# Gate/up stage of a transformer layer: a fourth seven-product pair, and one chunk split by a GpSimd DMA

## The chip, the cores and the metric

One core of a Trainium2 chip runs the whole layer as one program. The metric is the device time of one execution in microseconds. The engines are TensorE (PE; its weight loads are shown as PEld), VectorE (DVE), ScalarE (ACT), GpSimd (POOL) and SyncE (SP, here only the issuer of loads). They run side by side and wait for each other on semaphores.

## What is computed

The reference, cut to the stages that matter here. There are 256 tokens (two blocks of 128), D = 2048 and D_FF = 5632, all in float32.

```python
x = x + y @ w_out                       # out stage, y from the token mixing
h = rms_norm(x, ffn_norm)
x = x + (silu(h @ w_gate) * (h @ w_up)) @ w_down
return rms_norm(x, final_norm)
```

## The kernel before

**Products.** Every float32 operand is split in two: `hi`, its value rounded by a copy into a reduced float32 form, and `lo`, what is left. A product of 128 x 128 by 128 x 512 is three matmuls: hi by hi, hi by lo, lo by hi (`group`, L1571).

**Chunks and blocks.** Weights stream in chunks of 1 MB, `[128, 4, 512]`. The gate/up stage is 11 blocks (`FS`, index i), one for each 512 hidden columns; a block is 8 chunks (`FB`, index p), one for each pair of 128-row tiles of D. A chunk holds two row tiles of the up and of the gate matrix. The down stage has 44 chunks of the same size. Chunks are counted in one numbering, the gate/up stage from `FF0` and the down stage from `DN0`.

**Plain and seven-product chunks.** A plain chunk (`plain_chunk`) is 8 products, 24 matmuls, into the four PSUM banks 0 to 3: bank 2 up + b for token block b and matrix up or gate. A chunk in `SUMS` = 0, 2, 4 (`sums_chunk`) treats its four blocks as a 2 x 2 block product by the seven-product scheme, 21 matmuls. It needs four sums of weight blocks (`t_sum`, three DVE instructions), their hi and lo parts (`t_hi` by ACT, `t_lo` by DVE) beside the chunk's own three blocks, and seven blocks of x and its sums in place of four. Its shared products collect in banks 4 to 7. After the last chunk of `SUMS` these are combined (`mix_sums`) and added into banks 0 and 1, then 2 and 3 (`mix_banks(i, 0, ..)` and `mix_banks(i, 1, ..)`).

**Order in a block.** The matmuls of chunk `SUMS[-1]` signal `mix_done`; the plain chunk after it (5) does banks 0 and 1 first and signals `part_done`, and `mix_banks(i, 0)` waits for that; `mix_banks(i, 1)` waits for that chunk's end. Chunk 6 waits for `mixed` before each half. The last chunk ends the banks one by one (`ffn_done`). ACT turns banks 0 and 1 into `silu` (L811), DVE multiplies with banks 2 and 3 (L1354, the gate products). PE transposes the 128 x 512 results four tiles at a time (`hidden_turn`, L1463): the first group after the next block's chunk 0, the second after a quarter of its chunk 1. ACT copies each group into `hid` (`keep_hidden`, L769); the second group waits for the first copy.

**Preparation.** Each engine works through its list in order. At step p of block i ACT (`prep_hi`) and DVE (`prep_lo`) prepare chunk p + 3 (`AHEAD`): ACT makes `w_hi` from `raw` (and `t_hi` once the sums exist); DVE makes, for a plain chunk, `w_lo` = raw - w_hi (L1159), and for a sums chunk three sums (L1167, L1170, L1172), `w_lo` of three blocks (L1177) and `t_lo` (L1180). On DVE `mix_sums` and `mix_banks(i, 0)` stand at the head of step 4, `mix_banks(i, 1)` at the head of step 5, the gate products at the head of step 7. In the last block, steps 5 to 7 prepare the first chunks of the down stage (`down_lo`, L1296 to L1332). So at the end of a block DVE's list is: first bank mix, chunk 7, second bank mix, next chunk 0, next chunk 1, gate products, next chunk 2.

**Loads.** SP issues one load for a chunk into one of four buffers (`RING`), chunk n into `raw[n % 4]`, once chunk n - 4 is used (`chunk_used`, counted by PE). `w_lo` overwrites `raw`. `lo_ready` tells PE that a chunk is prepared. The residual x lies in `xin` (16 KB of each partition) from the in stage to the end; the out stage adds to it, `residual` reads it late in each half of the down stage. SP, DVE and ACT run the middle blocks in loops (`Fori`), PE too; out and down stage are written out.

## Time and profile before

| | us |
|---|---|
| median of 3 runs (1095.08 to 1096.28) | 1096.15 |
| the profiled execution, its own time | 1096.81 |
| its span, first to last instruction | 1095.1 |
| PE busy | 1084.2 |
| DVE busy | 886.2 |
| ACT busy | 617.8 |
| gate/up stage, by the chain | 387.56 to some 855 |

The span and the profiled execution's own time differ by 1.7 us, which lie around the program. PE's matmuls overlap in the record: each is shown with 0.39 us, but one starts every 0.23 us, so starts are what to read. In a timeline a row is one instruction or several alike; the bracket at its end is the idle time before it, with what ended it. Instructions on one engine can overlap by about 0.1 us, so the cost in a sequence is from one start to the next. In the chain in order of time a piece is a stretch of work on one engine and line.

### The profile page before, as it was taken

What the parts mean: (1) busy time and instruction counts of PE and PEld (TensorE: products, weight loads), DVE (VectorE), ACT (ScalarE), POOL (GpSimd) and SP (SyncE); (2) the same over time, 40 slices, a digit from 0 to 9 for tenths busy, and PEclk for the clock granted to TensorE, in tenths of its full rate; (3) what the DMA queues carried; (4) which work ended last, traced back from release to release, by engine and by line L of the source; (5) the groups of instructions that cost most, each with busy time, mean ns of one, the idle gap of its engine ahead of it and who ended that gap; (6) DMA issues with size and microseconds to landing.
All of it is one profiled execution on the core that took longest, in us unless ns stands there. A gap on an engine that the chain in (4) does not pass through costs nothing.

```text
span 1095.1 us, 13280 instructions
## 1 busy us (share of the span) xinstructions
PE 1084.2 (99%) x5127; PEld 902.5 (82%) x5127; DVE 886.2 (81%) x822; ACT 617.8 (56%) x616; POOL 44.5 (4%) x44
## 2 busy tenths in 40 slices
PE   9999999999999999999999999999999999999997
PEld 6888889987888888888888888888888888878886
DVE  7879666754576789898898898888898898989994
ACT  7666546655755655464554555554554765555553
POOL 0077000000000000000000000000000000000000
PEclk9999999999999999999999999999999999999999
DMA  8765644654355555555555555555555655555552
GB/s 329 282 232 194 199 137 124 202 159 147 118 192 169 178 197 211 200 198 192 192 194 198 208 189 207 192 192 196 198 214 197 230 193 197 202 194 204 202 193 114
DMA packets 48550, 212.57 MB, mean 194 GB/s; under 512 B 4096, under 2 KB 9984, under 8 KB 28544
## 3 DMA queue, kind: packets, MB, share of 16 engines
q1 hardware_dynamic: 47648, 209.65, 54.9%
q10 hardware_dynamic: 864, 2.39, 0.6%
q8 instruction: 27, 0.44, 0.2%
q14 instruction: 11, 0.09, 0.0%
HBM read 209.93 MB, written 2.10 MB: 194 GB/s over the span
## 4 chain that ended last, share of the span: by engine, by line
PE 96%; DVE 1%; DMA 1%; ACT 1%; issue 0%; SPq 0%; DVEq 0%
PE ps L1571 73%; PE ps L1424 6%; PE ps L1426 6%; PE ps L1425 6%; PE ps L1463 2%; DMA raw<-in_w_dn 1%; PE ps L1511 1%; PE ps L1688 1%; PE ps L1689 1%; PE ps L1690 1%; PE ps L1510 0%; DMA raw<-in_w_i 0%; DVE w_lo L1296 0%; ACT t_hi L788 0%; ACT w_hi L781 0%
## 5 line engine op out<-in xcount | busy, mean ns | idle before, releaser
L1571 PE MATMUL ps<-w_hi,xp_hi 128*128 128x512 f32 x539 | 211.7, 393 | 0.0
L1571 PE MATMUL ps<-w_hi,xp_lo 128*128 128x512 f32 x539 | 210.0, 390 | 0.0
L1571 PE MATMUL ps<-w_lo,xp_hi 128*128 128x512 f32 x539 | 209.7, 389 | 0.0
L887 DVE TENSOR_TENSOR w_lo<-raw,w_hi 128x2048 fp32r<-128x2048 f32 (+2 forms) x42 | 87.3, 2078 | 85.5 <-ACT w_hi L444 85.5
L1159 DVE TENSOR_TENSOR w_lo<-raw,w_hi 128x2048 fp32r<-128x2048 f32 x55 | 125.8, 2288 | 34.4 <-ACT w_hi L692 34.4
L692 ACT ACTIVATE w_hi<-raw 128x2048 fp32r<-128x2048 f32 x55 | 105.1, 1910 | 62.1 <-DMA raw<-in_w_gu 62.1
L781 ACT ACTIVATE w_hi<-raw 128x2048 fp32r<-128x2048 f32 (+1 forms) x44 | 79.2, 1800 | 80.0 <-DMA raw<-in_w_dn 79.9
L700 ACT ACTIVATE t_hi<-t_sum 128x2048 fp32r<-128x2048 f32 x33 | 63.4, 1920 | 100.0 <-DVE t_sum L1172 100.0
L1571 PEld LDWEIGHTS ps<-w_hi,xp_lo 128*128 128x128 f32 x539 | 101.1, 188 | 21.5
L1571 PEld LDWEIGHTS ps<-w_lo,xp_hi 128*128 128x128 f32 x539 | 101.3, 188 | 20.4
L1571 PEld LDWEIGHTS ps<-w_hi,xp_hi 128*128 128x128 f32 x539 | 101.2, 188 | 20.1
L1571 PE MATMUL ps<-w_hi,xo_hi 128*128 128x512 f32 x292 | 114.0, 390 | 0.4 <-DVE xin L1385 0.4
L1571 PE MATMUL ps<-w_lo,xo_hi 128*128 128x512 f32 x292 | 113.6, 389 | 0.0
L1571 PE MATMUL ps<-w_hi,xo_lo 128*128 128x512 f32 x292 | 113.6, 389 | 0.0
L444 ACT ACTIVATE w_hi<-raw 128x2048 fp32r<-128x2048 f32 (+2 forms) x42 | 73.0, 1738 | 49.5 <-DMA raw<-in_w_out 25.6
L1296 DVE TENSOR_TENSOR w_lo<-raw,w_hi 128x2048 fp32r<-128x2048 f32 x32 | 73.2, 2288 | 8.7 <-ACT w_hi L781 8.7
L1180 DVE TENSOR_TENSOR t_lo<-t_sum,t_hi 128x2048 fp32r<-128x2048 f32 x33 | 75.7, 2293 | 3.8 <-ACT t_hi L700 1.0
L696 ACT ACTIVATE w_hi<-raw 128x1536 fp32r<-128x1536 f32 x33 | 49.2, 1491 | 37.5 <-DMA raw<-in_w_gu 37.1
L1571 PEld LDWEIGHTS ps<-w_hi,xo_hi 128*128 128x128 f32 x292 | 54.8, 188 | 12.7 <-DVE xin L1385 0.8
L1571 PEld LDWEIGHTS ps<-w_hi,xo_lo 128*128 128x128 f32 x292 | 54.8, 188 | 11.4
L1571 PEld LDWEIGHTS ps<-w_lo,xo_hi 128*128 128x128 f32 x292 | 54.8, 188 | 11.1
L1571 PE MATMUL ps<-w_hi,xT_hi 128*128 128x512 f32 x156 | 60.9, 390 | 1.2 <-DVE w_lo L1017 1.0
(280 smaller groups left out, 2188.1 us busy)
## 6 DMA issues: line engine op xcount, KB each, us to landing
raw<-in_w_gu SPq DMA_DIRECT2D x88, 1024.0 KB, 4.8
raw<-in_w_dn SPq DMA_DIRECT2D x44, 1024.0 KB, 4.8
raw<-in_w_i SPq DMA_DIRECT2D x21, 1024.0 KB, 4.8
raw<-in_w_out SPq DMA_DIRECT2D x16, 1024.0 KB, 5.0
raw<-in_w_in SPq DMA_DIRECT2D x12, 1024.0 KB, 5.0
raw<-in_w_in SPq DMA_DIRECT2D x8, 576.0 KB, 3.8
raw<-in_w_i SPq DMA_DIRECT2D x6, 512.0 KB, 6.8
raw<-in_w_ukv SPq DMA_DIRECT2D x3, 1024.0 KB, 5.1
```

The source lines that it names most:

```text
L444: nc.scalar.activation(w_hi[n % 4][:, 0:k, 0:c], raw[n % 4][:, 0:k, 0:c], ACT.Copy).then_inc(hi_ready, 1)
L692: nc.scalar.activation(w_hi[slot][:], raw[slot][:], ACT.Copy).then_inc(hi_ready, 1)
L700: nc.scalar.activation(t_hi[s % 2][:], t_sum[s % 2][:], ACT.Copy).then_inc(tops_hi, 1)
L781: nc.scalar.activation(w_hi[slot][:, blocks, :], raw[slot][:, blocks, :], ACT.Copy).then_inc(hi_ready, 1)
L887: nc.vector.tensor_tensor(w_lo[n % 4][:, 0:k, 0:c], raw[n % 4][:, 0:k, 0:c], w_hi[n % 4][:, 0:k, 0:c].bitcast(F32), ALU.subtract).then_inc ...
L1159: nc.vector.tensor_tensor(w_lo[slot][:], raw[slot][:], w_hi[slot][:].bitcast(F32), ALU.subtract).then_inc(lo_ready, 1)
L1180: nc.vector.tensor_tensor(t_lo[s][:], t_sum[s][:], t_hi[s][:].bitcast(F32), ALU.subtract).then_inc(lo_ready, 1)
L1296: nc.vector.tensor_tensor(w_lo[slot][:], raw[slot][:], w_hi[slot][:].bitcast(F32), ALU.subtract).then_inc(lo_ready, 1)
L1424: nc.tensor.matmul(out, hi, w_h, start=start, stop=False)
L1425: nc.tensor.matmul(out, hi, w_l, start=False, stop=False)
L1426: return nc.tensor.matmul(out, lo, w_h, start=False, stop=stop)
L1571: mm = nc.tensor.matmul(out, x, wt, start=start and j + m == 0, stop=stop and 3 * j + m == n - 1, skip_group_check=resumed)
```

## The change

- `SUMS` becomes 0, 2, 4, 5. The last sums chunk is 5, chunk 6 is the one with `part_done`, and chunk 7 waits for `mixed` and ends the banks, all four in the order 0, 1, 2, 3. The sums of x for pair 5 are made in the out stage, with a fourth step in `XS_SPLIT`.
- Chunk 7 leaves the ring of four buffers and the lists of `prep_hi` and `prep_lo`. SP loads it into `d_raw` (`load_apart`, behind the load of chunk 3; in block 0 behind that of chunk 5). ACT (`prep_apart`, after step 2; in block 0 after step 3) copies it into `d_hi` and writes the negated `d_hi` over `d_raw`, in two halves, as `d_lo`. GpSimd then adds the same weights from DRAM onto `d_lo` by two accumulating DMAs of 512 KB, and PE waits for both (`lo_added`). Ring positions come from `ring(n)`, and a load waits for the last user of its buffer (`slot_user`).
- `d_lo` and `d_hi` lie on `xin`. SP writes x (2 MB) to `x_keep` in DRAM in block 0, behind the load of chunk 3, and reads it back in the down stage behind the load of its chunk 3; `residual` waits for `x_back`.
- On DVE `mix_sums` and `mix_banks(i, 0)` stand at step 5, then come the sums of the next chunk 0, `mix_banks(i, 1)`, and the low parts of that chunk. In the last block the whole `down_lo(0)` stands between the two. Chunk 5's sums wait for chunk 2's use.
- All loops of the stage are written out. Index arithmetic in `prep_*`, `down_*` and the PE functions follows `ring(n)`; it is left out below, as are the moved addresses of small tiles.

```diff
-SUMS = (0, 2, 4)
+SUMS = (0, 2, 4, 5)
 NS = len(SUMS)
+BY_DMA = 7
...
-for _step, _pairs in ((58, (0, 1)), (59, (2, 3)), (62, (4, 5)), (FF0, (6, 7))):
...
+for _step, _pairs in ((58, (0, 1)), (59, (2, 3)), (62, (4,)), (63, (5,)), (FF0, (6, 7))):
     put(_step, *(("xs2" if _pair in SUMS else "xt2", _pair) for _pair in _pairs))
-XS_SPLIT = {59: 0, 60: 1, 63: 2}
+XS_SPLIT = {59: 0, 60: 1, 63: 2, 64: 3}
...
+def ring(n):
+
+    return n - sum(FF0 + BY_DMA + FB * i < n for i in range(FS))
...
+def slot_user(n):
+
+    r = ring(n) - RING
+    return next(m for m in range(n) if ring(m) == r and not (FF0 <= m < DN0 and (m - FF0) % FB == BY_DMA))
...
+        d_raw = at("d_raw", 96 * K, [KC, COLS])
+        d_lo = at("d_lo", 96 * K, [KC, COLS], F32R)
+        d_hi = at("d_hi", 104 * K, [KC, COLS], F32R)
...
-            with sp.Fori(0, FS) as i:
+            def load_ring(n, src):
+
+                sp.wait_ge(chunk_used, slot_user(n) + 1)
+                sp.dma_start(raw[ring(n) % 4][:].rearrange("p a b -> p (a b)").unsqueeze(1), src).then_inc(raw_in[ring(n) % 4], 16)
...
+            def load_apart(i):
+
+                if i == 0:
+                    sp.wait_ge(x_kept, 16)
+                    sp.wait_ge(unit_filled, len(ORDER))
+                    sp.wait_ge(nx2.squared, 8)
+                else:
+                    sp.wait_ge(chunk_used, FF0 + FB * i)
+                sp.dma_start(d_raw[:].rearrange("p a b -> p (a b)").unsqueeze(1),
+                             w_gu[:, FB * i + BY_DMA:FB * i + BY_DMA + 1, :]).then_inc(d_in, 16)
+
+            for i in range(FS):
                 for p in range(FB):
-                    load_rows(i * FB + (FF0 + p), (FF0 + p) % 4, w_gu[:, bass.ds(i * FB + p, 1), :])
-            with sp.Fori(0, HKT // 4) as i:
-                for p in range(4):
-                    load_rows(i * 4 + (DN0 + p), (DN0 + p) % 4, w_dn[:, bass.ds(i * 4 + p, 1), :])
+                    if p != BY_DMA:
+                        load_ring(FF0 + FB * i + p, w_gu[:, FB * i + p:FB * i + p + 1, :])
+                    if i == 0 and p == 3:
+                        sp.wait_ge(acc_free, ACC_O + 8)
+                        sp.dma_start(t["x_keep"], xin[:].rearrange("p a b -> p (a b)")).then_inc(x_kept, 16)
+                    if p == (5 if i == 0 else 3):
+                        load_apart(i)
+            for m in range(HKT):
+                load_ring(DN0 + m, w_dn[:, m:m + 1, :])
+                if m == 3:
+                    sp.wait_ge(chunk_used, DN0)
+                    sp.dma_start(xin[:].rearrange("p a b -> p (a b)"), t["x_keep"]).then_inc(x_back, 16)
...
+            for i in range(FS):
+                for half in range(2):
+                    pool.wait_ge(negated, 2 * i + half + 1)
+                    pool.dma_start(d_lo[:, 2 * half:2 * half + 2, :].rearrange("p a b -> p (a b)"),
+                                   w_gu[:, FB * i + BY_DMA, 2 * COLS * half:2 * COLS * (half + 1)],
+                                   accum_op=ALU.add).then_inc(lo_added, 16)
...
+            def prep_apart(i):
+
+                act.wait_ge(d_in, 16 * (i + 1))
+                nc.scalar.activation(d_hi[:], d_raw[:], ACT.Copy).then_inc(d_hi_made, 1)
+                act.wait_ge(d_hi_made, i + 1)
+                for half in (slice(0, 2), slice(2, 4)):
+                    nc.scalar.activation(d_lo[:, half, :], d_hi[:, half, :].bitcast(F32), ACT.Copy,
+                                         scale=-1.0).then_inc(negated, 1)
...
-                    if p == 4:
+                    if p == SUMS[-1]:
...
-                            act.wait_ge(ffn_done, i * 3 + (2 * b + 1))
+                            act.wait_ge(ffn_done, i * 3 + (b + 1))
...
-                    else:
+                    elif p + AHEAD != BY_DMA:
                         prep_hi(i, p + AHEAD)
+                    if p == (3 if first else 2):
+                        prep_apart(i)
...
-            with act.Fori(1, FS - 1) as i:
+            for i in range(1, FS - 1):
...
                 if "s" in parts:
-                    dve.wait_ge(raw_in[slot], i * (4 * FB) + 16 * (n // 4 + 1))
+                    dve.wait_ge(raw_in[slot], 16 * (r // 4 + 1))
+                    if p == SUMS[-1]:
+                        dve.wait_ge(chunk_used, i * FB + (FF0 + SUMS[1] + 1))
...
-                    if p == 4:
+                    if p == SUMS[-1]:
                         mix_sums(i)
                         mix_banks(i, 0, None)
-                    if p == 5:
-                        mix_banks(i, 1, i * FB + (FF0 + 6))
                     if p == FB - 1:
                         for b in range(TOK):
                             dve.wait_ge(gate_set, i * 2 + (b + 1))
                             if b == 0:
-                                dve.wait_ge(ffn_done, i * 3 + 2)
+                                dve.wait_ge(ffn_done, i * 3 + 3)
                             else:
                                 dve.wait_ge(chunk_used, i * FB + (FF0 + FB))
                             nc.vector.scalar_tensor_tensor(out=gate[:, b, :], in0=bank[2 + b],
@@ -1356,7 +1419,13 @@
                                                            op0=ALU.mult, op1=ALU.mult).then_inc(hid_made, 1)
                     if last and p + AHEAD >= FB:
                         down_lo(p + AHEAD - FB)
-                    else:
+                        if p == SUMS[-1]:
+                            mix_banks(i, 1, i * FB + (FF0 + 7))
+                    elif p == SUMS[-1]:
+                        prep_lo(i, p + AHEAD, "s")
+                        mix_banks(i, 1, i * FB + (FF0 + 7))
+                        prep_lo(i, p + AHEAD, "l")
+                    elif p + AHEAD != BY_DMA:
...
                 if half == 0:
                     dve.wait_ge(mix_step, 3 * i + 3)
+                    dve.wait_ge(x_back, 16)
...
-                slot = (FF0 + p) % 4
+                w_h, w_l = (d_hi, d_lo) if p == BY_DMA else (m[ring(FF0 + FB * i + p) % 4] for m in (w_hi, w_lo))
...
-                sides = ((0, 0), (1, 0), (0, 1), (1, 1)) if p in (5, 6) else ((0, 0), (0, 1), (1, 0), (1, 1))
+                sides = ((0, 0), (1, 0), (0, 1), (1, 1)) if p > SUMS[-1] else ((0, 0), (0, 1), (1, 0), (1, 1))
                 for g, (b, up) in enumerate(sides):
                     if p == 1 and g == 1:
                         sums_chunk(i, 0, True, late=True) if first else hidden_turn(i, 1)
                     if p == 1 and g == 3:
                         if not first:
                             pe_.wait_ge(hid_kept, i * 2)
-                    if p == 6 and g % 2 == 0:
+                    if p == SUMS[-1] + 2 and g % 2 == 0:
                         pe_.wait_ge(mixed, i * 2 + (g // 2 + 1))
                     toks = slice(b * P, (b + 1) * P)
                     cols = (1, 3) if not up else (0, 2)
                     mm = group(bank[2 * up + b], [xp_hi[p][:, j, toks] for j in range(2)],
-                               [xp_lo[p][:, j, toks] for j in range(2)], [w_hi[slot][:, j, :] for j in cols],
-                               [w_lo[slot][:, j, :] for j in cols], p == 1 and g == 3, p in (5, FB - 1), resumed=p > 5)
-                    if p == 5 and g == 1:
+                               [xp_lo[p][:, j, toks] for j in range(2)], [w_h[:, j, :] for j in cols],
+                               [w_l[:, j, :] for j in cols], p == 1 and g == 3, p > SUMS[-1], resumed=p == SUMS[-1] + 2)
+                    if p == SUMS[-1] + 1 and g == 1:
                         mm.then_inc(part_done, 1)
...
-                    pe_.wait_ge(lo_ready, i * FB + (FF0 + p + 1))
+                    if p == BY_DMA:
+                        pe_.wait_ge(lo_added, 32 * (i + 1))
+                    else:
+                        pe_.wait_ge(lo_ready, ring(FF0 + FB * i + p) + 1)
```

## Rows read from the trace of the kernel before

**Rows 1.** The page, the chain that ended last, by engine.

```profile
PE 96%; DVE 1%; DMA 1%; ACT 1%; issue 0%; SPq 0%; DVEq 0%
```

**Rows 2.** The chain in order of time: start us, us, what.

```profile
519.77 0.44 PE ps L1463 x4
...
522.11 40.15 PE ps L1571 x177
...
562.26 0.44 PE ps L1463 x4
...
862.17 93.20 PE ps L1571 x411
```

**Rows 3.** Timeline of PE: start us, us, engine, line, operation, count.

```profile
1.25 4.90 PE L1561 MATMUL ps<-warm 128*128 128x512 bf16 x14 [1.25 <-DVE warm L922]
...
541.02 0.39 PE L1571 MATMUL ps<-w_hi,xp_hi 128*128 128x512 f32 x1
...
557.34 0.39 PE L1571 MATMUL ps<-w_hi,xp_hi 128*128 128x512 f32 x1
```

**Rows 4.** Windows: us, busy time of each engine, granted clock, DMA share, GB/s.

```profile
10.00:20.00 10.00, 10.00 (x46) 8.29 (x45) 7.39 (x9) 7.61 (x11) 0.00 (x0) 1.00 1.04 409
510.00:550.00 40.00, 40.00 (x182) 32.98 (x181) 34.76 (x26) 20.92 (x16) 0.00 (x0) 1.00 0.56 200
1088.00:1089.00 1.00, 0.17 (x1) 0.00 (x0) 0.07 (x1) 0.69 (x2) 0.00 (x0) 1.00 0.72 279
1090.00:1091.00 1.00, 0.00 (x0) 0.00 (x0) 0.68 (x1) 0.72 (x1) 0.00 (x0) 0.59 0.00 0
```

**Rows 5.** Waits, 429 to 856 us: who waited for whom, us, times, longest.

```profile
PEld ps L1463 <- ACT hid L769: 2.9, 10, 0.3
```

**Rows 6.** Timeline of DVE, out stage and gate/up stage.

```profile
371.96 2.29 DVE L887 TENSOR_TENSOR w_lo<-raw,w_hi 128x2048 fp32r<-128x2048 f32 x1 [3.14 <-ACT w_hi L444]
...
406.94 2.29 DVE L1159 TENSOR_TENSOR w_lo<-raw,w_hi 128x2048 fp32r<-128x2048 f32 x1
...
543.94 1.23 DVE L1283 TENSOR_TENSOR ps<-ps,mix 128x1024 f32<-128x1024 f32 x1 [1.14 <-PE ps L1571]
...
547.28 1.23 DVE L1283 TENSOR_TENSOR ps<-ps,mix 128x1024 f32<-128x1024 f32 x1
548.41 1.22 DVE L1167 TENSOR_TENSOR t_sum<-raw 128x1024 f32<-128x1024 f32 x1
...
550.39 0.69 DVE L1172 TENSOR_TENSOR t_sum<-t_sum,raw 128x512 f32<-128x512 f32 x1
...
555.28 2.29 DVE L1159 TENSOR_TENSOR w_lo<-raw,w_hi 128x2048 fp32r<-128x2048 f32 x1
557.48 1.40 DVE L1354 SCALAR_TENSOR_TENSOR gate<-ps,stats,gate 128x512 f32<-128x512 f32 x2
```

**Rows 7.** Timeline of DVE, last gate/up block, where it prepares the down stage.

```profile
846.00 1.22 DVE L1307 TENSOR_TENSOR t_sum<-raw 128x1024 f32<-128x1024 f32 x1
...
849.57 1.75 DVE L1325 TENSOR_TENSOR w_lo<-raw,w_hi 128x1536 fp32r<-128x1536 f32 x1
851.24 0.68 DVE L1327 TENSOR_TENSOR xo_lo<-hid,xo_hi 128x512 fp32r<-128x512 f32 x1
...
854.65 2.28 DVE L1296 TENSOR_TENSOR w_lo<-raw,w_hi 128x2048 fp32r<-128x2048 f32 x1
```

**Rows 8.** Timeline of ACT at the same block boundary as rows 6.

```profile
561.50 1.92 ACT L700 ACTIVATE t_hi<-t_sum 128x2048 fp32r<-128x2048 f32 x1 [2.92 <-DVE t_sum L1172]
563.32 0.58 ACT L769 ACTIVATE hid<-ps 128x512 f32 x1
```

**Rows 9.** The page, DMA issues: count, KB each, median us to landing.

```profile
raw<-in_w_gu SPq DMA_DIRECT2D x88, 1024.0 KB, 4.8
...
raw<-in_w_i SPq DMA_DIRECT2D x6, 512.0 KB, 6.8
...
xin<-in_x SPq DMA_DIRECT2D x2, 1024.0 KB, 7.0
```

More of the change, by code:

```diff
@@ L141, in build @@
             offset += 2 * size
-        H0 = 153 * K
+        H0 = 156 * K
         assert offset <= H0
@@ L686, in prep_hi @@
             def prep_hi(i, q, parts="bt"):
-                slot, p = (FF0 + q) % 4, q % FB
+                r, p = ring(FF0 + FB * i + q), q % FB
+                slot = r % 4
                 if "b" in parts:
-                    act.wait_ge(raw_in[slot], i * (4 * FB) + 16 * ((FF0 + q) // 4 + 1))
+                    act.wait_ge(raw_in[slot], 16 * (r // 4 + 1))
                 if p not in SUMS:
@@ L776, in down_hi @@
             def down_hi(m):
-                n, q, slot = DN0 + m, m % DQ, (DN0 + m) % 4
-                act.wait_ge(raw_in[slot], 16 * (n // 4 + 1))
+                r, q = ring(DN0 + m), m % DQ
+                slot = r % 4
+                act.wait_ge(raw_in[slot], 16 * (r // 4 + 1))
                 blocks = slice(1, 4) if q in DSUMS else slice(0, 4)
@@ L1367, in _ @@
             ffn(0, first=True)
-            with dve.Fori(1, FS - 1) as i:
+            for i in range(1, FS - 1):
                 ffn(i)
@@ L1742, in sums_chunk @@
                     if first and not late:
-                        after(unit_act, "a", ("xt2", 5))
-                        after(unit_dve, "v", ("xt2", 5))
+                        after(unit_act, "a", ("xs2", 5))
+                        after(unit_dve, "v", ("xt2", 3))
                     elif not first:
@@ L1807, in _ @@
             ffn(0, first=True)
-            with pe_.Fori(1, FS) as i:
+            for i in range(1, FS):
                 ffn(i)
@@ L1965 @@
         t[name] = nc.dram_tensor(f"in_{name}", a.shape, mybir.dt.from_np(a.dtype), kind="ExternalInput").ap()
+    t["x_keep"] = nc.dram_tensor("x_keep", (P, TOK * D), F32, kind="Internal").ap()
     t["out"] = nc.dram_tensor("out_0", (1, TOK * P, D), F32, kind="ExternalOutput").ap()
```

30 lines of the change are left out of this document (17 added, 13 removed).

## The prediction

> **What bounds the kernel now.** I read the page first, then the chain in order of time, the windows, the waits of the gate/up stage, and the timelines of TensorE (PE), VectorE (DVE) and ScalarE (ACT) over one block. By the chain that ended last PE is the bound, with 96% of it [rows 1]. In order of time, one gate/up block is four pieces, two of them transposes, the largest 177 matmuls in 40.15 us, and the next block begins 42.49 us after it [rows 2]. One matmul thus takes 40.15/177 = 0.2268 us. Chunk 5 starts at 541.02 and the next block's chunk 0 at 557.34 [rows 3]: three plain chunks in 16.32 us, 5.44 each; a seven-product chunk of 21 matmuls takes 4.76.
>
> How much room do the others have? In a stretch of 40 us DVE is busy 34.76 and ACT 20.92 [rows 4]. An average hides the order, so I look at the waits: ten times, at every block boundary, the second group of hidden-layer transposes (L1463) waits up to 0.3 us for ACT's copy `hid` (L769) [rows 5]. That is the one chain of this stage with no room at all: DVE's gate product, DVE's three sums for chunk 2, ACT's `t_hi`, ACT's `hid` copy, PE's second turn. It sits where the change puts DVE's work later.
>
> **The matmuls removed.** Chunk 5 of 11 blocks goes from 24 matmuls to 21: 33 x 0.2268 = 7.5 us off the path.
>
> **DVE's total.** Start to start, a sums chunk costs DVE 6.87 us (548.41 to 555.28), a plain one 2.20 (555.28 to 557.48) [rows 6]. The change adds the sums chunk 5 and takes away the plain chunks 5 and 7: 6.87 - 4.40 = 2.5 us more. Before, a block needs 3 x 6.87 + 5 x 2.20 + some 5 for the mixes + 1.3 for the gates = 37.9; after, 40.4 of 41.8 us. As a total that fits. The order decides.
>
> **The order, before.** DVE's first bank mix starts at 543.94, 2.92 us into chunk 5, released by the end of that chunk's first half [rows 3, 6]. I call this the event. From there DVE has no gap: bank mix 1.13, chunk 7's split 2.20, bank mix 1.13, sums chunk 0 6.87, plain chunk 1 2.20; the two gate products start at 557.48 [rows 6], 13.54 us after the event. The event lies 16.32 - 2.92 = 13.40 us before the next chunk 0, so the gates start 0.14 us after it.
>
> **The order, after.** The last sums chunk is now 5 and the event lies in chunk 6, 10.88 - 2.92 = 7.96 us before the next chunk 0. DVE then has: bank mix 1.13; the next chunk 0's sums, 1.98 for the first two (548.41 to 550.39) and 0.60 for the third (0.69 less the 0.09 by which followers overlap), 2.58; bank mix 1.13; chunk 0's low parts, 1.67 (849.57 to 851.24, the same form without a wait) + 2.20 = 3.87; plain chunk 1 2.20 [rows 6, 7]. Sum 10.91: the gates start 2.95 us after the next block's nominal start, **2.8 us later** than before. The work in the chain fell by 2.6 us, its start moved by a whole chunk of 5.44.
>
> **What the 2.8 us meets.** Chunk 0's low parts end 8.8 us after the event, where PE wanted them at 7.96: it waits 0.9 us there. Then the tight chain: from the gates' start to the `hid` copy it is 5.84 us (557.48 to 563.32) [rows 6, 8], with no room [rows 5]. So the whole 2.8 us lands in front of PE's second turn, the 0.9 being part of it and some 2 us a second gap. Does DVE catch up before the next event? From the gates it needs 1.3 + 6.87 + 2.20 + 6.87 + 6.87 + 2.20 = 26.3 us and ends 29.3 us after the nominal start of chunk 0; chunk 6 starts at 2.8 + 41.8 - 10.9 = 33.7. Yes, so the delay doesn't grow. What is late next, behind the turn, is nothing. Ten boundaries: **10 x 2.81 = +28.1 us**.
>
> **The last block.** Here the code doesn't part the sums from the low parts: `down_lo(0)` runs whole between the two bank mixes. It took from 846.00 to 854.65, 8.65 us [rows 7], but behind both mixes. Now the second mix ends 1.13 + 8.65 + 1.23 = 11.0 us after the event, and PE needs it for the second half of chunk 7, at 2.52 + 2.72 = 5.24. PE stands still for **5.8 us**, once. The down stage can't give it back: its first chunks had no PE wait before.
>
> **The clock.** At the tail PE's last matmul ends at 1088.17 (0.17 us busy in that window); between 1090 and 1091 the granted clock is 0.59, on its way from 2.4 to 1.2 GHz [rows 4]. A gap of 5.8 us should lose the clock too. To get it back I take the start: 14 matmuls of 512 columns took 4.90 us [rows 3] against 14 x 0.2268 = 3.18: **+1.7 us**. For the boundary gaps I take none; that is rival (a).
>
> **The first block.** Chunk 5's sums follow chunk 4's on DVE, at 406.94 [rows 6]; with 6.87 and the overlap they end at 413.9, where chunk 5 would start at 557.34 - 3 x 42.49 - 16.32 = 413.5: **+0.4**. In the SP queue 2 MB of x go to DRAM ahead of the loads of chunks 4 to 6, from about 388 on. At 409 GB/s, the most in a window [rows 4], that is 5 us and hidden; at twice the 7.0 us of 1 MB of x [rows 9] it is 14 us, chunk 4's load lands near 405 and it costs up to 5. I take the first: one transfer with long rows, like the weight loads, which land in 4.8 us.
>
> **Costed at nothing.** GpSimd's accumulating DMA: no row shows one. ACT's work for it stands behind chunk 5's `t_hi`. Counted from chunk 6's start, DVE begins chunk 5's sums at 13.8 + 1.3 + 6.87 + 2.20 + 6.87 = 31.1; `t_hi` ends at 31.1 + 2.7 + 1.9 = 35.7 [rows 8], `d_hi` at 37.6, the first negation near 38.7; PE wants the next chunk 7 at 44.6 + 5.4 = 50.1, 11.4 us later. From below, 1 MB lands in 4.8 us; from above, two transfers of 512 KB in series take 2 x 6.8 = 13.6 [rows 9]. Even that is 2.2 us late, and up to 2.8 us at chunk 7 only shorten the gap behind it. So 0, and free up to 14 us. Nothing is queued behind GpSimd's waits. ACT's added work, about 1.9 for `d_hi`, 2.2 for two negations and 1.9 for another `t_hi`, lies beside its idle half; its nearest cover is chunk 6's split behind it, with 0.6 us left. The written-out loops: 177 matmuls took 40.15 in a loop, 411 took 93.20 in the straight down stage [rows 2], both 0.2268: 0. Pair 5's sums of x give DVE and ACT 1 to 2 us more in the out stage, where DVE waited 3.14 us at one step [rows 6]: 0. Reading x back: 0, at most 4 if it takes 14 us and holds up a load of the down stage. DVE's new wait for chunk 2 ends over 1 us before DVE gets there.
>
> The Trainium skill, "DMA: Bandwidth & Descriptors", "Anatomy of one DMA", gives a GpSimd DMA some 2 us plus its bytes over 436 GB/s. That makes an estimated 3.2 us for a half, and the sum stays as it is; no run here shows one yet.
>
> **The sum.** -7.5 + 28.1 + 5.8 + 1.7 + 0.4 = +28.5. On the profiled execution's 1096.8 that is 1125.3; the median of the runs lies 0.66 lower: **1125**.
>
> **Rivals.** (a) The clock falls at every boundary gap as well. For: it was going some 2 us into the tail. Against: matmuls part the 0.9 from the 2. Price 10 x 1.7 = 17: **1142**. (b) The accumulating DMA is slow. Its halves have 14 us; each microsecond beyond costs 11 in all, so at 18 us **1169**. Against: the DMA engines are used 0.56 in this stage [rows 4]. (c) The other side, faster: DVE reaches the gates in time. It decides at 8.1 us from the event to the gates in place of 10.9; then only the matmuls count, 1096.2 - 7.5 = **1089**. For: DVE's total fits. Against: DVE would have to be a quarter quicker than its rows. (d) Turn and copy have slack I don't see and hide half: -7.5 + 14 + 7.5 + 0.4, **1111**.
>
> The Trainium skill, "SBUF — State Buffer", section "SBUF: two separate sides", says that GpSimd can't write descriptors while DVE runs in a two-port mode, which would be a road to (b). The same page says that two-input subtractions have no such mode, and DVE's rows here are of that kind, so (b) stays small.
>
> **Chances.** Forecast 0.68, (a) 0.13, (b) 0.07, (c) 0.07, (d) 0.05. The forecast's own range is 1120 to 1135: below, no clock loss and 0.3 us less at each boundary; above, +5 and +4 for the two transfers of x. To hold 8 in 10 it must reach to (a): 1116 to 1142. A measurement of this kernel tells about 0.2% from no change. Faster 0.07, same 0.01, slower 0.92.
>
> **What would show it.** Right: about 2 us of PE idle before the second turn, ended by ACT `hid`, and 0.9 before chunk 0, ended by DVE `t_lo`; one gap near 5.8 us in the last block, ended by DVE's bank mix; blocks of 44.6 us against 42.49; and only there a lower granted clock. Wrong: blocks of 41.8 us, or PE waiting at chunk 7 for GpSimd's DMA. The prediction falls if the gates start within 0.3 us of the next chunk 0.

## The result and the profile after

The changed kernel takes 1152.7 us in the median of 4 runs (1150.75 to 1156.22), beside 1095.88 for the kernel before on the same chip: a ratio of 1.0522, 95% interval [1.0500, 1.0545], some 57 us slower. (A ratio here is always the kernel's time over that of the kernel before, and the brackets behind it are its 95% interval.) The forecast was 1125, with 1116 to 1142 as the range. The direction was right, but half the size was missing: the time is some 11 us above the range. The profiled execution of the changed kernel has a span of 1150.7 us.

From the page of the changed kernel: busy time by engine, the chain that ended last, and of the DMA part the two queues (packets, MB, share of 16 engines) and one issue (count, KB each, median us to landing).

```profile
PE 1098.2 (95%) x5094; PEld 906.2 (79%) x5094; DVE 911.0 (79%) x858; ACT 653.4 (57%) x650; POOL 69.8 (6%) x66
...
PE 64%; DVE 10%; ACT 10%; DMA 9%; issue 6%; POOL 1%; SPq 0%; DVEq 0%; ACTq 0%
...
q1 hardware_dynamic: 47936, 213.84, 54.6%
q0 software_dynamic: 3168, 11.54, 5.6%
...
d_lo<-in_w_gu POOLq DMA_DIRECT2D x22, 512.0 KB, 8.2
```

PE had 96% of the chain before [rows 1]; now it has 64, and all the others stand in it. No total but PE's is near full, and PE's 95% overstates it, since its matmuls overlap in the record and some ran at the lower clock (below). A chain that runs through every engine while none of the others is full suggests a loop: each waits for the one before it. The waits of the gate/up stage, 429 to 932 us, say who (us in total, times, longest; a selection, not in the order of the view):

```profile
PE ps L1641 <- DMA d_lo<-in_w_gu: 37.6, 11, 5.6
PEld ps L1641 <- DVE w_lo L1221: 7.9, 10, 0.8
PE ps L1641 <- DVE w_lo L1221: 3.6, 10, 0.4
POOL d_lo L480 <- issue: 38.6, 5, 7.9
PE ps L1641 <- DVE ps L1347: 0.3, 1, 0.3
PEld ps L1533 <- ACT hid L818: 0.2, 1, 0.2
```

The wait on which most of my sum stood, PE's second turn for ACT's `hid` (L1533, the line of [rows 5] in the old numbering), is there once, with 0.2 us. In its place PE waits for the accumulating DMA in each of the 11 blocks. Blocks, from chunk 7 to chunk 7, are some 47 us in the second half of the stage (716.59 to 763.49 is one) and 46.8 to 49.9 in the first; all ten take 475.3 us (428.54 to 903.81). I had 44.6 for one; before they were 42.49 [rows 2].

The chain in order of time over one block (start us, us, what; pieces of `issue` of 0.02 us are left out without a mark), with the DMA and chunk 7 of the block behind it:

```profile
683.55 0.45 PE ps L1533 x4
684.03 0.60 ACT hid L818
684.63 1.81 ACT w_hi L741
...
686.46 2.29 DVE w_lo L1221
688.75 1.15 DVE t_sum L1231
...
695.53 1.23 DVE t_sum L1231
...
698.24 1.92 ACT t_hi L749
700.16 1.81 ACT d_hi L845
701.99 1.07 ACT d_lo L848
703.06 0.38 issue
703.44 0.85 POOL d_lo L480
704.29 12.25 DMA d_lo<-in_w_gu
716.54 0.04 issue
716.59 10.52 PE ps L1641 x45
...
728.94 0.45 PE ps L1533 x4
...
749.75 7.86 issue
757.61 5.84 DMA d_lo<-in_w_gu
...
763.49 12.00 PE ps L1641 x45
```

Read it as a circle: PE's second turn, ACT's second `hid` copy, ACT's `w_hi` of chunk 3 queued behind it, DVE's split of chunk 3, the sums of chunks 4 and 5, `t_hi`, `d_hi`, the first negation, GpSimd's issue, 12.25 us of DMA, chunk 7, and PE's second turn again. From turn to chunk 7 it takes 716.59 - 683.39 = 33.2 us (the turn's start in PE's timeline), from there to the next turn 12.2. Together that is 45.4 us, the period of this block: a lateness on the circle comes round to the engine that was late, so nothing absorbs it.

The block behind it shows two things that make the circle longer. GpSimd's second half is issued only after 7.86 us of `issue`, that is, of waiting for nothing that the profile shows. And the 45 matmuls from chunk 7 on take 12.00 us in place of 10.52, because the first of them run at a lower clock.

### The profile page after: what moved, and what is told of

The parts are those of the page before. It is cut to its first block, busy times and chain, and to the rows that moved or that the text cites. A ratio compares the mean times of both kernels' runs of the same rounds, so it can differ in the third digit from the quotient of the medians.

```text
span 1150.7 us, 12406 instructions
## 1 busy us (share of the span) xinstructions
PE 1098.2 (95%) x5094; PEld 906.2 (79%) x5094; DVE 911.0 (79%) x858; ACT 653.4 (57%) x650; POOL 69.8 (6%) x66
## 3 DMA queue, kind: packets, MB, share of 16 engines
q0 software_dynamic: 3168, 11.54, 5.6%
## 4 chain that ended last, share of the span: by engine, by line
PE 64%; DVE 10%; ACT 10%; DMA 9%; issue 6%; POOL 1%; SPq 0%; DVEq 0%; ACTq 0%
PE ps L1641 43%; DMA d_lo<-in_w_gu 8%; PE ps L1494 5%; PE ps L1496 5%; PE ps L1495 5%; ACT t_hi L749 4%; DVE w_lo L1221 3%; DVE t_sum L1231 2%; ACT w_hi L741 2%; PE ps L1533 2%; ACT d_hi L845 2%; DVE t_sum L1236 1%; DVE t_sum L1234 1%; ACT d_lo L848 1%; POOL d_lo L480 1%
## 5 line engine op out<-in xcount | busy, mean ns | idle before, releaser
L1641 PE MATMUL ps<-w_hi,xp_hi 128*128 128x512 f32 x396 | 157.4, 397 | 4.2 <-DVE w_lo L1221 3.6
L1641 PE MATMUL ps<-w_lo,xp_hi 128*128 128x512 f32 x396 | 154.5, 390 | 0.0
L1641 PE MATMUL ps<-w_hi,xp_lo 128*128 128x512 f32 x396 | 154.4, 390 | 0.0
L1221 DVE TENSOR_TENSOR w_lo<-raw,w_hi 128x2048 fp32r<-128x2048 f32 x33 | 75.5, 2289 | 51.4 <-ACT w_hi L741 51.4
L1641 PEld LDWEIGHTS ps<-w_hi,xp_hi 128*128 128x128 f32 x396 | 74.3, 188 | 23.5 <-DVE w_lo L1221 7.9
L1361 DVE TENSOR_TENSOR w_lo<-raw,w_hi 128x2048 fp32r<-128x2048 f32 x32 | 73.2, 2286 | 12.3 <-ACT w_hi L831 12.3
L1641 PE MATMUL ps<-d_hi,xp_hi 128*128 128x512 f32 x88 | 42.2, 480 | 37.9 <-DMA d_lo<-in_w_gu 37.6
L1241 DVE TENSOR_TENSOR w_lo<-raw,w_hi 128x1536 fp32r<-128x1536 f32 x44 | 77.3, 1756 | 1.1
L1641 PE MATMUL ps<-t_hi,xp_hi 128*128 128x512 f32 x176 | 68.5, 389 | 0.4 <-DVE xp_lo L1190 0.4
L1641 PE MATMUL ps<-t_hi,xp_lo 128*128 128x512 f32 x176 | 68.5, 389 | 0.0
L1641 PE MATMUL ps<-t_lo,xp_hi 128*128 128x512 f32 x176 | 68.5, 389 | 0.0
```

Of the source, the lines that this page charges most:

```text
L1221: nc.vector.tensor_tensor(w_lo[slot][:], raw[slot][:], w_hi[slot][:].bitcast(F32), ALU.subtract).then_inc(lo_ready, 1)
L1241: nc.vector.tensor_tensor(w_lo[slot][:, 1:4, :], raw[slot][:, 1:4, :], w_hi[slot][:, 1:4, :].bitcast(F32), ALU.subtract)
L1361: nc.vector.tensor_tensor(w_lo[slot][:], raw[slot][:], w_hi[slot][:].bitcast(F32), ALU.subtract).then_inc(lo_ready, 1)
L1641: mm = nc.tensor.matmul(out, x, wt, start=start and j + m == 0, stop=stop and 3 * j + m == n - 1, skip_group_check=resumed)
```

## The experiments

The kernel before, measured again beside each run, took 1095.5 to 1096.5 us. In the code, `...` marks what is left out.

### Without the accumulating DMA

```diff
-                for half in range(2):
-                    pool.wait_ge(negated, 2 * i + half + 1)
-                    pool.dma_start(d_lo..., w_gu..., accum_op=ALU.add)
...
-                        pe_.wait_ge(lo_added, 32 * (i + 1))
+                        pe_.wait_ge(negated, 2 * (i + 1))
```

> The changed kernel without GpSimd's two accumulating DMAs; PE waits for the negation instead. Left out: chunk 7's low part is only -hi, so that chunk's product is wrong. Theory A (the DMA, 13.5 us from the first negation to the data, lies in a closed loop turn 2, hid copy, w_hi, DVE chunks 3, 4, 5, t_hi, d_hi, DMA, chunk 7, turn 2; but DVE's order alone costs as predicted): blocks of about 45 us, PE waits again at the second turn, time 1126 to 1131. Theory B (the DMA is the whole loss; DVE's new order costs nothing by itself): blocks of 41.8 us, 1090 to 1094. Theory C (the DMA's latency hardly matters, its traffic or the chunk set apart does): stays above 1140.

Measured: 1132.84 us, ratio 1.0332 [1.0311, 1.0352]. The DMA is worth 1152.7 - 1132.8 = 20 us of the 57. The blocks are 45.3 us. Waits of that kernel:

```profile
PE ps L1527 <- ACT hid L812: 16.3, 10, 1.6
PE ps L1635 <- DVE t_lo L1238: 7.9, 11, 0.7
PE ps L1635 <- DVE ps L1341: 5.7, 1, 5.7
PE ps L1635 <- DVE w_lo L1215: 3.6, 10, 0.4
```

The first three rows are what the prediction named: the second turn late by `hid` (some 2), chunk 0 late by `t_lo` (0.9), one gap in the last block (5.8). The fourth it did not: chunk 6's split, for which it left ACT 0.6 us, comes 0.4 us late ten times. It also shows that the place of the negations alone, without any DMA behind them, makes blocks of 45.3 us and not 44.6.

### The same DMA without the addition

```diff
-                                   accum_op=ALU.add).then_inc(lo_added, 16)
+                                   ).then_inc(lo_added, 16)
```

> The same two DMAs, same bytes, same queue and same waits, but they overwrite in place of adding. Left out: chunk 7's low part is the weight itself, so its product is wrong. Theory A1 (adding is what makes the DMA slow, since it reads its target too): the two halves land in 5 to 7 us and the time is that of e1 within 3 us. Theory A2 (descriptors made by GpSimd, or its small ring, are slow): 10 us or more to landing, the second one still issued 7.7 us late in some blocks, time within 5 us of 1152.

Measured: 1134.53 us, 1.0347. The same bytes by the same queue to the same place cost about what no transfer costs; PE waits for it twice, 3.1 us in all. From its page, beside the rows of after above:

```profile
q0 software_dynamic: 3168, 11.54, 2.9%
...
d_lo<-in_w_gu POOLq DMA_DIRECT2D x22, 512.0 KB, 6.1
```

Adding doubles the DMA engines' time for the same 11.54 MB, 2.9% to 5.6% of all 16, and lengthens a half from 6.1 to 8.2 us in the median. GpSimd's queue is the same in both, so it is the addition that makes the transfer too late here.

### The negations one step earlier

```diff
-                    if p == (3 if first else 2):
+                    if p == (3 if first else 1):
                         prep_apart(i)
```

> ACT splits and negates chunk 7 one step earlier, behind chunk 4 in place of chunk 5. Nothing is left out. By theory A the DMA starts about 7 us earlier and is in time; what is left is DVE's order: 1124 to 1129, PE waiting about 2 us at each second turn and not at chunk 7. By theory B 1090 to 1094. By theory C it stays above 1140.

Measured: 1129.78 us, 1.0299 [1.0282, 1.0316]: 23 us for one line, with nothing else touched. Its waits:

```profile
PE ps L1533 <- ACT hid L818: 14.7, 9, 1.6
PE ps L1641 <- DVE t_lo L1244: 7.1, 10, 0.7
PE ps L1641 <- DVE ps L1347: 5.7, 1, 5.7
PE ps L1641 <- DMA d_lo<-in_w_gu: 3.1, 1, 3.1
```

PE waits for the DMA only in block 0, where the negations kept their place, and the block is 44.7 us (444.64 to 489.33, from behind one second turn to behind the next), where the prediction had 44.6. This is the kernel that I predicted; the changed kernel would have been it, had the negations stood one step earlier.

### VectorE's order repaired

```diff
                     if p == SUMS[-1]:
+                        dve.wait_ge(chunk_used, i * FB + (FF0 + 5))
+                        prep_lo(i, FB, "s")      # next chunk 0's sums
                         mix_sums(i)
+                        prep_lo(i, FB, "w")      # its w_lo
                         mix_banks(i, 0, None)
...
-                        prep_lo(i, p + AHEAD, "s")
-                        mix_banks(i, 1, i * FB + (FF0 + 7))
-                        prep_lo(i, p + AHEAD, "l")
+                        prep_lo(i, FB, "t")      # its t_lo
+                        mix_banks(i, 1, i * FB + (FF0 + 7))
```

On ACT, `w_hi` of the next chunk 3 goes ahead of `t_hi` of chunk 2; the last block is parted in the same way, and the negations stand as in the run above.

> e3, and DVE's list around the end of a block put in another order: the next chunk 0's three sums ahead of the mix sums, its own low part ahead of the first bank mix, its sums' low part between the two bank mixes; ACT makes chunk 3's w_hi ahead of chunk 2's t_hi; the same in the last block. Theory A: DVE's gates start with the next chunk 0 again and every boundary wait goes: blocks of 41.8 to 42.0 us, 1089 to 1094. Rival D (DVE's total, 40.3 of 41.8 us, is too tight once it waits at all): blocks of 42.5 to 43.5 us, 1096 to 1108, with PE waiting for DVE's w_lo or t_lo.

Measured: 1110.35 us, 1.0129 [1.0105, 1.0152]. The waits at the turn are gone, 19 us with them, but the kernel is still 14 us above the one before. Blocks, chunk 7 to chunk 7, are 41.9 to 44.5 us, without a pattern. In a long one, from the chain in order of time, and from the waits:

```profile
497.25 8.17 DMA raw<-in_w_gu
...
505.52 1.24 DVE t_sum L1235
...
512.36 1.23 DVE ps L1352
```

```profile
DVE t_sum L1235 <- DMA raw<-in_w_gu: 22.9, 9, 4.3
PE ps L1664 <- DVE ps L1352: 14.7, 12, 2.9
```

The load of the next chunk 0 took 8.17 us beside the accumulating DMA, where the loads of this stage had a median of 4.8 before [rows 9]. DVE waited with the sums, the bank mix behind them came late, and PE waited for it.

### The negations as early as they can go

```diff
-                    if p == (3 if first else 1):
+                    if p == (1 if first else 0):
                         prep_apart(i)
```

> e4, with ACT's split of chunk 7 one step earlier still (step 0; in block 0 step 1). In e4 the load of the next chunk 0 took 8.2 us to land in the slow blocks, in place of 4.8, beside the accumulating DMA. Theory A: the DMA is nearly through when that load is issued; blocks of 41.8 us nearly everywhere, 1089 to 1095. Rival E (the accumulating DMA slows whatever load lies beside it, and there is always one that matters): slow blocks stay, 1100 to 1112.

Measured: 1112.82 us, 1.0159 [1.0144, 1.0175]. The long loads are still there (up to 10.1 us); PE's wait for the bank mixes is 15.0 us in place of 14.7, in 20 pieces in place of 12. Nothing is won by moving it.

### Chunk 7 apart, the sums as before

```diff
-SUMS = (0, 2, 4, 5)
+SUMS = (0, 2, 4)
```

The mixing stands at its old steps; the accumulating DMA and the spill of x stay.

> The change without its fourth seven-product pair: chunk 7 apart, accumulating DMA and x spilled as in the change, ACT's split behind chunk 5, but SUMS = 0, 2, 4 and the mixes where they were. Theory A (closed loop): from PE's second turn to the data 27.8 us, to chunk 7 30.4 us, so the DMA is in time and nothing waits: 1094 to 1100. Rival F (the DMA and the spill cost some 4 to 5 us a block by themselves, wherever they are): 1140 or more.

Measured: 1099.71 us, 1.0029 [1.0019, 1.0038]. This half of the change costs some 3 us by itself; in its profiled execution, at 1101.95 us, one wait for a bank mix in block 0 is 3.8 us, and the blocks from the fifth on are 42.4. The DMA is as slow as in the changed kernel (8.7 us in the median), but DVE has one sums chunk less, the transfer has some 16 us from the first negation to chunk 7 (457.2 to 473.3 in one block), and no matmul waits for it.

### Loops written out

```diff
-            with act.Fori(1, FS - 1) as i:
+            for i in range(1, FS - 1):
```

The same on DVE, PE and SP (and SP's loop over the down stage), in the kernel before.

> The kernel before with the loops of the gate/up and down stages written out on all engines, nothing else. The forecast costed this at 0: 1095 to 1097. Rival G (more instructions to fetch cost or spare something): over 2 us away.

Measured: 1096.42 us, 1.0000 [0.9991, 1.0009]. It was costed at nothing, and it costs nothing that shows.

### Without the store of x

```diff
-                        sp.dma_start(t["x_keep"], xin...).then_inc(x_kept, 16)
...
-                    sp.dma_start(xin..., t["x_keep"]).then_inc(x_back, 16)
+                    sp.dma_start(xin[:], x_v).then_inc(x_back, 16)
```

> e5 without the 2 MB store of x in block 0; the later read takes the input x in its place. Left out: the out stage's part of the residual, so the result lacks it. The forecast costed the store at 0, at most 5 us: by it this is within 1 us of e5. Rival: 3 us or more below e5, with block 0 shorter.

Measured: 1114.46 us against 1112.82 with the store (base: the negations as early as they can go). The 2 MB going out cost nothing: the kernel without them is 1.6 us slower in the median, and the runs of both overlap (1112.88 to 1117.07, 1112.62 to 1116.04).

### The repaired order: with the DMA away, plain, or in one piece

The next four runs ask what keeps the repaired order 14 us above the kernel before. The first differs from the repaired order in two things, the DMA and the negations, which stand where the changed kernel has them.

> The order of e4 (next chunk 0's sums ahead of the mixing, ACT's split of chunk 3 ahead of t_hi of chunk 2), but both accumulating DMAs left out, so that d_lo holds minus the high part and chunk 7's low products are false; PE waits for ACT's negations. Theory (the accumulating DMA costs e4 its last 15 to 20 us, by making the 1 MB loads beside it late): without it the load of the next chunk 0 lands within 5 us again, no wait of VectorE for it over 1 us, blocks of 41.8 us throughout, 1089 to 1094 us, under the kernel before. Rival D (VectorE's order is too tight by itself): PE still waits for the mixing of the banks, 1100 us or more.

Measured: 1111.67 us, 1.0143. DVE waited 34.3 us, 11 times, for ACT's split of chunk 6 behind the negations. Read alone it would have cleared the DMA. Beside the next run it says only that, without a DMA, the negations' place costs the repaired order 20 us. The clean run, the repaired order with the two DMAs away and nothing else:

> e4 exactly (the negations one step early, the order of e4), with only the two accumulating DMAs left out: d_lo holds minus the high part, so chunk 7's low products are false, and PE waits for the negations. It is what e9 was meant to be; e9 also had the negations at the step of the changed kernel, and VectorE waited 34.3 us for ACT's split of chunk 6 behind them. Theory (the accumulating DMA is worth e4's last 15 to 20 us): blocks of 41.8 us throughout, VectorE's waits for raw<-in_w_gu under 3 us, 1089 to 1095 us. Rival D (VectorE and ACT together are too tight for any order, DMA or not): 1105 us or more, as e9.

Measured: **1091.32 us**, 0.9963 [0.9949, 0.9977], blocks of 41.7 us. Against the repaired order with the DMA that is 19 us. Its waits:

```profile
DVE t_sum L1229 <- DMA raw<-in_w_gu: 3.9, 9, 1.0
...
PEld ps L1658 <- DVE ps L1346: 1.6, 2, 0.9
```

And between the two, the DMA there but without the addition:

> e4 with the addition dropped from both GpSimd DMAs: they overwrite d_lo with the raw rows, so the low products of chunk 7 are false; the bytes and their place are the same. If it is the adding that slows the loads beside it (twice the engine time per byte), the load of chunk 0 lands in about 5 us and the time is 1090 to 1096 us. If it is any transfer beside the load, or the GpSimd queue, it stays at 1105 us or more.

Measured: 1096.19 us, 0.9997 [0.9988, 1.0007]. Of the 19 us some 5 are for having a 1 MB transfer beside the loads at all, 14 for its adding. The load of chunk 0 is late here too, but by less than the order forgives:

```profile
DVE t_sum L1234 <- DMA raw<-in_w_gu: 17.4, 9, 2.9
...
PE ps L1663 <- DVE ps L1351: 5.0, 10, 0.8
```

DVE's nine waits average 1.9 us and reach PE with 0.5; in the adding kernel they average 2.5, up to 4.3, and reach it with 1.2, up to 2.9. By the longest of each (2.9 against 0.8, 4.3 against 2.9) the slack ahead of the bank mix is an estimated 1.4 to 2.1 us; a wait beyond it reaches PE.

One accumulating DMA of 1 MB in place of two halves:

> e4 with one accumulating DMA of 1 MB behind both negations in place of two of 512 KB. Rival (the queue's place for descriptors, which held the second half's issue back by up to 7.9 us): a single DMA issues at once or is itself held; if holding was what spread the contention over the load of chunk 0, the landing of that load changes by over 1 us and the time goes to under 1104 us. Theory (bytes added in memory are the load on the engines, however cut): the one DMA takes 10 to 14 us and the time stays within 1105 to 1115 us.

Measured: 1117.3 us, 1.0193. It lands in 8.7 us, sooner than 10 to 14, and the time is above the range of either theory. So the late issue of second halves, which held five of the eleven in the changed kernel back by up to 7.9 us, is not what the repaired order pays for: without it DVE's wait for chunk 0's load grew from 22.9 to 29.5 us. The run also starts the whole transfer later, behind both negations, so it doesn't tell what the cut alone does.

### Two other orders

Mixing ahead of the next chunk 0's sums:

```diff
+                        mix_sums(i)
                         prep_lo(i, FB, "s")
-                        mix_sums(i)
                         prep_lo(i, FB, "w")
                         mix_banks(i, 0, None)
```

> e4, the DMA in, with one step moved: mix_sums (2.6 us) ahead of the next chunk 0's sums, so that a load of chunk 0 that lands up to 3 us late is waited for behind work that needed doing anyway. In e4's slow block ACT's copy for the mixing ended at 631.01 and VectorE stood idle for the load until 633.39; mixing first puts the first bank mix at about 638 instead of 640.23, ahead of PE's chunk 7 at 639.9. Theory: VectorE's waits for raw<-in_w_gu fall from 22.9 us to under 8, PE's for the bank mixes (14.7 + 4.6 us) to under 4, and the time is 1090 to 1098 us, level with the kernel before or a little under it. Rival E (the contention finds another load): 1105 us or more.

Measured: 1113.45 us, 1.0164: a miss. DVE's wait for that load is gone, as expected, but the blocks are 43.5 us. Timeline of DVE:

```profile
640.66 0.69 DVE L1337 TENSOR_TENSOR mix<-mix,ps 128x512 f32<-128x512 f32 x1 [2.91 <-PE ps L1664]
...
643.25 1.21 DVE L1235 TENSOR_TENSOR t_sum<-raw 128x1024 f32<-128x1024 f32 x1
...
647.63 1.23 DVE L1352 TENSOR_TENSOR ps<-ps,mix 128x1024 f32<-128x1024 f32 x1
```

`mix_sums` can't start before PE ends chunk 5. I had taken ACT's copy for that end, 1.5 us too soon. From there to the end of the first bank mix DVE works 8.2 us where PE has the 5.4 of chunk 6: a new circle, with a wait in every block in place of one in some. The other way, mixing and the first bank mix ahead of the sums:

> e4, the DMA in, with mix_sums and the first bank mix ahead of the next chunk 0's sums, the second bank mix behind them and w_lo and t_lo last. In e10 one block was 43.5 us because from the end of PE's chunk 5 VectorE worked 2.6 (mix_sums) + 2.6 (sums) + 1.7 (w_lo) + 1.2 us to the first bank mix, 8.1 us where PE has 5.4 us of chunk 6. Here the bank mix is ready after 3.8 us, and t_lo of the next chunk 0 after 11.7 us where PE has chunks 6 and 7, 10.9 us: 0.8 us late in each of 11 boundaries. Theory: PE waits for t_lo some 0.8 us instead of for the bank mixes, blocks of 42.6 us, 1096 to 1102 us. Rival E (the late loads find the chain again): 1105 us or more.

Measured: 1127.24 us, 1.0288, a miss too. That bank mix waits for the first half of chunk 6, which I had forgotten, and DVE stood idle for it eleven times, 21.5 us in all. Timeline of DVE:

```profile
599.69 0.69 DVE L1337 TENSOR_TENSOR mix<-mix,ps 128x512 f32<-128x512 f32 x1 [2.48 <-PE ps L1659]
...
604.38 1.23 DVE L1352 TENSOR_TENSOR ps<-ps,mix 128x1024 f32<-128x1024 f32 x1 [2.01 <-PE ps L1659]
```

With 2.0 us idle there and 2.5 before it, the late turn of 1.6 us comes back, 9 times. DVE needs some 40 of a block's 41.8 us, which leaves no room for 4.5 us of idle time; blocks are 44.7 us.

### Chunk 7's low part on GpSimd

In the repaired order:

```diff
-                    pool.wait_ge(negated, 2 * i + half + 1)
-                    pool.dma_start(d_lo..., w_gu..., accum_op=ALU.add)
+                pool.wait_ge(d_hi_made, i + 1)
+                nc.gpsimd.tensor_tensor(d_lo[:], d_raw[:], d_hi[:].bitcast(F32), ALU.subtract)...
```

ACT's two negations go as well.

> e4's order and e3's early step, but chunk 7's low part is made as the other plain chunks' is, d_lo = d_raw - d_hi, by one subtraction on GpSimd in place; ACT's two negations and both accumulating DMAs go. Nothing is left out. From GpSimd's own rows (a 128x192 multiply in 0.508 us, a 128x192 subtraction in 1.444 us) the 128x2048 subtraction takes 5.4 to 15.4 us; it may start when d_hi is made, some 20 us before PE's chunk 7. Theory (with the DMA gone nothing makes the loads late, as e13): blocks of 41.8 us, 1089 to 1095 us, under the kernel before. Rival G (GpSimd's subtraction makes VectorE's rows longer or comes late to chunk 7): VectorE's 128x2048 subtraction over 2.4 us beside it, or a wait of PE for d_lo, and 1100 us or more.

Measured: 1130.66 us, 1.0312 [1.0298, 1.0326]. Rival G came true. Timelines of GpSimd and DVE:

```profile
632.56 4.91 POOL L479 TENSOR_TENSOR d_lo<-d_raw,d_hi 128x2048 fp32r<-128x2048 f32 x1 [39.74 <-ACT d_hi L842]
```

```profile
626.05 1.22 DVE L1228 TENSOR_TENSOR t_sum<-raw 128x1024 f32<-128x1024 f32 x1
...
632.92 5.63 DVE L1228 TENSOR_TENSOR t_sum<-raw 128x1024 f32<-128x1024 f32 x1
```

The same DVE instruction takes 1.22 us, and 5.63 when it starts within GpSimd's 4.91: it ends about 1.1 us after GpSimd does (638.55 and 637.47), so it did its whole work behind it. DVE's busy time is 956.6 us against 909.1, or 4.3 us for each of 11 blocks, in which it had under 2 us to spare; the blocks are 44.1 to 46.3 us. The Trainium skill, "SBUF — State Buffer", section "SBUF: two separate sides", says that a GpSimd instruction that reads SBUF and a DVE instruction with two inputs in SBUF take a shared port pair as an exclusive lock, each for its whole instruction. The trace agrees, with these numbers.

## Why the prediction was right or wrong

**Matmuls removed, -7.5: right.** 5094 matmuls against 5127 are in the page, and the repaired order without the DMA, which takes most of the waits away, gains 4.2 us on the one before (1091.32 against 1095.55 beside it). From the second on its blocks are 41.74 us against 42.49, 0.75 less, where three matmuls are 0.68.

**DVE's order, +28.1: right, but not in this kernel.** Without the DMA, or with the negations earlier, the gaps are the named ones (`hid` 1.6, `t_lo` 0.7); the block is 44.7 us for 44.6 with the negations early, and 45.3 without the DMA, where chunk 6's split is late as well. In the changed kernel it is hidden: PE is late at chunk 7 instead.

**The last block, +5.8: right in its parts, hidden in the sum.** `down_lo(0)` took 8.64 us between the bank mixes (898.49 to 907.13; I had 8.65), and the gap was 5.7 wherever PE was otherwise in time. In the changed kernel most of it lies beside the wait for the DMA, and 0.3 us of wait is left.

**The clock, +1.7: right in the last block.** Behind the gap of 5.67 us, in the kernel with the earlier negations, eight matmuls start 0.43 us apart in place of 0.23: 8 x 0.2 = 1.6 us.

**The accumulating DMA at 0: the step that failed.** Two sizes of it held. I had 11.4 us from the first negation to PE's chunk 7; it was 10.9 (703.06 to 713.97, 2.62 us before chunk 7's start at 716.59, where PE's idle time starts). I had 13.6 us as the upper bound of the transfer; it took 13.5 where both halves were issued at once (0.38 for the signal, 0.85 issue, 12.25 landing), and 15.0 in a block where the second was held back (748.46 to 763.45, in the chain in order of time). I chose the lower end, 4.8, from loads on another queue that do not add. The upper bound would have led to the same 0, because of the sentence "up to 2.8 us at chunk 7 only shorten the gap behind it". That sentence is false. It takes DVE's lateness for a fixed time; but DVE's gates wait for PE's banks at chunk 7 (16.2 us in the changed kernel), and DVE's split of chunk 3 waits for ACT behind the second `hid` copy, which waits for PE's turn. Of two circles through a block the longer sets the period, and the shorter vanishes in it. The DVE circle is 44.6 by the forecast and 45.3 with the negations in this kernel's place. The one through the DMA is 45.4 where both halves are issued at once and the clock stays up (33.2 + 12.2), and 48.5 where the second is held back and the clock falls behind the gap (34.7 + 13.8).

The ten blocks take 475.3 us where ten of mine are 446, 29 us more. The pieces of the chain part them, as an estimate: 8 us are the circle at its shortest (10 x 0.8), and by the run without the DMA they would be there without it too; some 13 are matmuls at the lower clock behind PE's wait at chunk 7; some 7 are second halves that were issued late (in four of the ten blocks, 1.0 to 2.9 us each). The first block adds 4 us to this, and the gap of the last block, of whose 7.5 us 5.6 are hidden, takes them off again: 27 to 28, as measured. So the circle alone would have made the forecast 1133, within its range. What carried the time out of it are two things that the forecast had not put at PE's wait for the DMA: the clock, which rival (a) had at another gap, and GpSimd's late issue, which it had nowhere. Both cost time only while PE waits for that DMA: with the earlier negations second halves are still issued late (5 times, 25.9 us), and the kernel is 23 us faster.

The link was in the trace of before: DVE's idle 1.45 us at 524.69, ended by ACT's `w_hi`, in the middle of the stretch in which I had DVE catch up at its own pace. Timeline of DVE, kernel before:

```profile
524.69 2.29 DVE L1159 TENSOR_TENSOR w_lo<-raw,w_hi 128x2048 fp32r<-128x2048 f32 x1 [1.45 <-ACT w_hi L692]
```

By the figure of the Trainium skill, "DMA: Bandwidth & Descriptors", "Anatomy of one DMA", a half was an estimated 3.2 us. Measured were 5.3 to 6.1 in the median for a plain one and 5.8 to 8.9 for an adding one, two of them sharing the time; the measurement decides.

**Rival (b)** named the DMA and priced it at 11 us for each microsecond beyond 14. The mechanism held; the point from which it decides was wrong, as just told: the circle passes 44.6 at 13.5 - 0.8 = 12.7 us, and from the first negation to the data it took 13.4 to 16.4 in the blocks behind the first. **Rival (a)**, the clock at each boundary gap, fell in its place and came true in another. Behind the gaps of 1.6 us in the earlier-negation kernel matmuls follow at their full pace. Behind those at chunk 7 it varies: gaps of 2.62 and 2.65 us cost nothing, gaps of 2.70, 2.56 and 4.13 us some eight matmuls at 0.43 us, which is 1.2 GHz in place of 2.4: some 8 x 0.2 = 1.6 us each, near the 1.7 I had for one. Nine of the eleven gaps at chunk 7 cost this. A window of the changed kernel, behind the gap that ends at 669.59 (us; busy times; clock; DMA share; GB/s):

```profile
671.00:674.50 3.50, 3.50 (x11) 2.69 (x10) 3.50 (x2) 1.99 (x4) 0.00 (x0) 0.52 0.20 82
```

Why a gap of 2.56 us costs the clock and one of 2.65 does not stays open. **(c)** and **(d)** fell: DVE's gates were late, and where the DMA is out of the way the gaps have their full size.

**The first block, +0.4: too small.** Chunk 7 of block 0 starts at 428.54, against 424.36 in the kernel before and 424.1 by the forecast (413.5 + 0.4 + 4.76 + 5.44). It waited 3.2 us for the same DMA (3.1 in the earlier-negation kernel, whose matmuls behind it are slow as well). That, and 0.1 us a block, makes most of what parts my 1125 from its 1129.8. Chunk 5, to which the 0.4 belonged, waited 0.5 us for DVE's `t_lo`.

**ACT's added work at 0: too small.** The cover of 0.6 us for chunk 6's split was gone: 0.4 us of wait ten times, and blocks of 45.3 us in place of 44.7 where no DMA stands in the way. In the repaired order, which has less room, the same place costs 20 us. **Loops and the store of x: right**, by a run each. The reading back of x has no run of its own; it landed within 8.1 us, and behind it the down stage shows no wait of PE.

**The whole, step by step** from the kernel before to the changed one, in the order in which the runs part it: matmuls and the repaired order without a DMA -4.6; the DMA's load on its neighbours +19.0; VectorE's order +19.4; the negations one step late +22.9; together +56.8. In another order the parts would differ, since they hide one another. A kernel that beats the one before and leaves nothing out was not found: the low part of chunk 7 costs more than the 4 to 5 us that the matmuls give, by an accumulating DMA (19) or on GpSimd (39).

What stays open: why one DMA of 1 MB, which lands sooner than two halves, costs 7 us more; what in an addition takes the engines' time twice; and what holds GpSimd's second half back. The kernels are all compiled with a scratch of 1024 bytes for GpSimd's DMA descriptors (`dynamic_dma_scratch_size`), and no run changed it.

## What to carry to other kernels

Before calling a lateness hidden, follow it once around the loop body: who waits next, and does any of it lead back to the engine that was late? If it closes, the lateness is paid in every turn, and the longest circle, not the sum of gaps, is the period. Then ask what the new wait brings with it: here the clock behind the wait cost an estimated 13 us, the circle itself 8. An operation that no row of the trace shows gets the far bound, not the near one, wherever its allowance is of the same size, and its effect on transfers beside it counts as well as its own time.

## What the runs showed of the hardware

- An accumulating DMA from DRAM into SBUF takes about twice the engine time of a plain one per byte (5.6% against 2.9% of the 16 engines for 11.54 MB), and a 1 MB load beside it landed in 8.17 us, where the median of the stage before was 4.8. DVE's waits for such a load were 22.9 us beside adding DMAs, 17.4 beside plain ones, 3.9 beside none.
- Of two accumulating DMAs of 512 KB in a row the second was issued up to 7.9 us late in 5 of 11 cases, after which it landed in 5.84 us (that of 757.61); the plain ones were held 4 times, for up to 6.0 us.
- Behind nine of eleven PE gaps of 2.6 to 5.6 us at chunk 7 some eight matmuls ran at 0.43 us; behind gaps of 2.62 and 2.65 us, and behind all of 1.6 us, none did.
- A GpSimd subtraction of 128x2048 of 4.91 us held a two-input DVE instruction, begun 0.36 us behind it, back by 4.4 us (5.63 for 1.22).
